# The last tile of a mixture-of-experts routing: turned once scaled, its copy shared with VectorE, four scatters moved behind the gathers, more turns of the identity

## What is computed

```python
x = x + (sigmoid(g_a) * y_attn + sigmoid(g_p) * y_pool) @ w_o
h = rmsnorm(x, g_ffn)                      # 1024 rows of 1024
logits = h @ w_router + b_router           # 32 experts
top_val, top_idx = top_k(logits, 4)        # each token goes to 4 experts
# tokens are grouped by expert; each expert's rows are gathered,
# go through gate/up, a clamped SwiGLU and down, and are added back by gate weight
```

## Time and profile before

| | |
|---|---|
| median of 3 runs | 2408.51 us (2408.11 to 2412.3) |
| the profiled execution | 2410.38 us |
| its span | 2408.7 us |
| TensorE busy | 2364.5 us, 98% of the span |
| VectorE busy | 1334.0 us, 55% |
| ScalarE busy | 460.3 us, 19% |
| GpSimd busy | 423.7 us, 18% |
| mean granted TensorE clock | 0.997 of full speed |

### The profile page before, as it was taken

How to read it: one execution, slowest core, us unless ns; L and a number is a source line. 1 busy time by engine, 2 the same in 40 slices (tenths; PEclk the granted TensorE clock), 3 DMA queues, 4 the chain that set the end, 5 groups by cost and what they waited for, 6 DMA issues and landing times. The chain is left out here.

```text
span 2408.7 us, 45402 instructions
## 1 busy us (share of the span) xinstructions
PE 2364.5 (98%) x15700; PEld 1611.2 (67%) x15700; DVE 1334.0 (55%) x2477; ACT 460.3 (19%) x1150; POOL 423.7 (18%) x589
## 2 busy tenths in 40 slices
PE   8999999999998999999999999999999999999999
PEld 6765664444444888888888888888656565555544
DVE  4665674111356654455545554556767677776565
ACT  3434552000022100000000000100212212121332
POOL 2451102121243310001100110010010101011230
PEclk9999999999999999999999999999999999999999
DMA  5000002312052798787888888888999999999462
GB/s 151 27 18 10 1 0 53 122 26 52 22 183 88 265 371 318 285 304 283 288 309 303 285 298 313 303 312 316 331 336 357 326 357 341 341 348 336 162 201 87
DMA packets 255033, 531.84 MB, mean 221 GB/s; under 512 B 17845, under 2 KB 67909, under 8 KB 254950
## 3 DMA queue, kind: packets, MB, share of 16 engines
q1 hardware_dynamic: 222302, 472.57, 55.0%
q0 software_dynamic: 17440, 38.97, 5.3%
q10 hardware_dynamic: 15208, 19.14, 2.2%
HBM read 498.76 MB, written 31.87 MB: 220 GB/s over the span
## 5 line engine op out<-in xcount | busy, mean ns | idle before, releaser
L1923 PEld LDWEIGHTS banks<-arena_a,arena_w 128*128 128x128 f32 x4608 | 562.9, 190 | 7.8 <-issue 6.5
L1923 PE MATMUL banks<-arena_a,arena_w 128*128 128x144 f32 (+7 forms) x4608 | 566.7, 286 | 1.0 <-ACT arena_a L2095 1.0
L1976 PE MATMUL banks<-arena_w,arena_a 128*64 128x256 f32 x2688 | 298.6, 380 | 3.0 <-DVE arena_a L2254 1.7
L1976 PEld LDWEIGHTS banks<-arena_w,arena_a 128*64 128x64 f32 x2688 | 193.3, 137 | 107.3 <-issue 14.1
L2349 DVE TENSOR_SCALAR arena_m<-banks,arena_m 128x160 f32<-128x160 f32 x144 | 55.3, 384 | 305.0 <-PE banks L1923 304.5
L1305 POOL DMA_DIRECT2D arena_m<-slot_tokens x32 | 18.8, 587 | 1024.9 <-issue 1024.9
L2150 ACT ACTIVATE arena_m<-arena_m 128x160 f32<-128x160 f32 x144 | 48.5, 337 | 785.7 <-DVE arena_m L2349 473.9
L1931 PE MATMUL banks<-arena_w,arena_a 128*64 128x256 f32 x1728 | 197.5, 381 | 0.0
L2032 PE MATMUL banks<-arena_w,arena_a 128*128 128x512 f32 x448 | 194.6, 592 | 0.0
L1931 PEld LDWEIGHTS banks<-arena_w,arena_a 128*64 128x64 f32 x1728 | 120.9, 137 | 67.6 <-issue 10.4
L2032 PEld LDWEIGHTS banks<-arena_w,arena_a 128*128 128x128 f32 x448 | 84.0, 190 | 100.4 <-issue 100.4
(11 more groups left out here) (410 smaller groups left out, 3443.2 us busy)
## 6 DMA issues: line engine op xcount, KB each, us to landing
arena_w<-in_w_gate_up_dram SPq DMA_DIRECT2D x128, 2048.0 KB, 12.7
arena_w<-in_w_down_dram SPq DMA_DIRECT2D x32, 4096.0 KB
expert_rows<-arena_a ACTq DMA_DIRECT2D x104, 128.0 KB, 8.6
arena_a<-in_x_dram SPq DMA_DIRECT2D x16, 512.0 KB, 4.8
arena_w<-in_w_in_dram SPq DMA_DIRECT2D x16, 512.0 KB, 5.4
arena_a<-in_b_down_dram SPq DMA_DIRECT2D x14, 512.0 KB, 15.3
expert_rows<-arena_a ACTq DMA_DIRECT2D x28, 192.0 KB
arena_a<-in_b_down_dram SPq DMA_DIRECT2D x72, 64.0 KB
```

The source lines that it names most:

```text
L1923: m = pe.matmul(GU[f % 3][:, to:to + width], w[c][:, k, at:at + P], xT[:, k, 0:width], start=(k == 0), stop=(k == K - 1), skip_group_check ...
L1976: m = pe.matmul(at[h * TH:(h + 1) * TH, :], x[:, k, :], w[:, k, h * QB:(h + 1) * QB], start=(start and k == 0), stop=(stop and k == KH - 1 ...
```

## The change

Five edits, all in the tail of routing.
1. TensorE turns the last tile (T-1) before the ranks of tile T-2, not after them.
2. For the last tile ScalarE copies only the first bank of turned rows. VectorE copies the second, between the choice and the rank of tile T-2.
3. Between the ranks of T-2 and the parts of T-1 TensorE makes ten more turns of the identity.
4. The four scatters of tile T-2 are taken out of routing's program and put behind the two gathers, together with those of T-1: two copies of token numbers, then eight indirect DMAs.
5. While the gathered rows come, TensorE makes 44 turns of the identity instead of 40.

```diff
@@ route, GpSimd
-                def scatter(n, last=False):
+                def scatter(n):
...
-                    if not last:
-                        pool.wait_ge(scattered, 64 * n + 64)
-                        pool.sem_inc(sem("dst_free"), 1)
+                    pool.wait_ge(scattered, 64 * n + 64)
+                    pool.sem_inc(sem("dst_free"), 1)
...
-                scatter(T - 2, last=True)
-
@@ route, TensorE
                 parts(T - 2)
                 logits(T - 2)
                 stay_warm(WARM // 2)
+                turn(T - 1)
                 ranks(T - 2)
-                turn(T - 1)
+                stay_warm(WARM // 4)
                 parts(T - 1)
                 logits(T - 1)
                 ranks(T - 1)
...
-                for _ in range(WARM):
+                for _ in range(WARM + WARM // 10):
                     pe.transpose(banks[0][:, 0:P], ident[:, :], ident[:, :])
@@ route, ScalarE, keep_rows
-                    for h, bank in enumerate((TB0, TB1)):
+                    for h, bank in enumerate((TB0, TB1)[:1 if n == T - 1 else 2]):
@@ route, VectorE
+                def keep_last_half():
+                    dve.wait_ge(sem("h2T_psum"), T)
+                    dve.tensor_copy(h2T[(T - 1) % 2][:, 4:8, :].rearrange("p k t -> p (k t)"), TB1[:, :]).then_inc(sem("h2T"), 1)
...
                 scale(T - 1)
                 choose(T - 2)
+                keep_last_half()
                 rank(T - 2)
                 place_rows(T - 2)
@@ experts, GpSimd
                 pool.wait_ge(route_sem("dst"), T)
-                pool.tensor_copy(tokb[1], tok[:, T - 1:T]).then_inc(sem("tokb"), 1)
-                pool.wait_ge(sem("tokb"), 1)
-                for j in range(TOP_K):
-                    pool.indirect_dma_start(list_dram, bass.IndirectOffsetOnAxis(dst[1][:, j:j + 1], 0), tokb[1], None
-                                            ).then_inc(scattered, 16)
+                for n in (T - 2, T - 1):
+                    pool.tensor_copy(tokb[n % 2], tok[:, tile_of(n):tile_of(n) + 1]).then_inc(sem("tokb"), 1)
+                pool.wait_ge(sem("tokb"), 2)
+                for n in (T - 2, T - 1):
+                    for j in range(TOP_K):
+                        pool.indirect_dma_start(list_dram, bass.IndirectOffsetOnAxis(dst[n % 2][:, j:j + 1], 0), tokb[n % 2], None
+                                                ).then_inc(scattered, 16)
                 pool.wait_ge(scattered, 64 * T)
                 pool.wait_ge(sem("table"), 32)
```

## The result

The changed kernel takes **2414.5 us** (median; 2410.46 to 2416.84), the kernel before, measured beside it, 2408.76 (2406.75 to 2412.3). The ratio is 1.0024 with a 95% interval of 1.0015 to 1.0033: it is slower by 5.7 us. The forecast was 2407.3, the range ended at 2410.3, and slower by over 0.2% had a chance of 0.04. The profiled execution takes 2413.5 us, its span is 2411.9; the mean granted clock is 0.998.

What follows compares the result with a forecast made beforehand. TensorE, busy 98%, bounds the kernel, but in routing's tail a chain of short steps over four engines does. 1.34 less 0.15 gave 1.2 us: 2408.51 - 1.2 = 2407.3 us, range 2405.2 to 2410.3.

Steps and rivals of the forecast that it cites:

- Steps 1, 2 and 3: Routing's tail: earlier turn, VectorE's half copy and ten identity turns let the last choice start 1.34 us sooner.
- rival (b): Parts of the last tile show the long lag to ScalarE's copy: gain only 0.8 us before turns, 2407.9; chance 0.2.
- Step 4: From last choice to indices nothing is removed: the 4.88 us chain moves as a whole, no clock gain counted.
- rival (d): Larger gain: clock holds through the choice (0.4 us), gather starts 0.55 sooner, turns end in time; 2406.2, chance 0.12.
- Step 5: Four scatters moved behind the gathers cost nothing, covered by GpSimd's wait for the item table and TensorE's first item.
- the step's own worst case: All scatters behind the gathers slow, landing at 812.7 us at the latest, some 2 us of the row-list wait left.
- Step 6: 44 identity turns while gathered rows come may end 0.3 us after the rows; half, 0.15 us, counted as loss.
- The sum: First expert matmul 1.2 us sooner (1.34 - 0.15), all passing through to the end: 2407.3 us.
- Whatever comes sooner at 798.98 comes sooner at the end: From the first expert matmul on, TensorE works solidly, so time won there reaches the end, and no more.
- (e): The eight scatters land so late that they reach item 1's row list: slower by several us, 2414; chance 0.03.
- (a): Clock falls again at the experts' start, in the wait for gathered rows: 2409.0, or 2412.4 if long; chance 0.15.
- (c): VectorE's copy comes at the wrong place or identity turns run over, giving back the turn's gain: 2408.5; chance 0.1.

Runs made afterwards that it cites:

- e0: The changed kernel again with no edit; 2413.75 us against 2407.75 for the kernel before, ratio 1.0026.
- e3: The changed kernel, but SyncE waits for all scatters to land before issuing the load of expert 0's second half; 2416.84 us, ratio 1.0045 to the kernel before.
- e7: The changed kernel with the item table sent by ScalarE's queue and the w_down load following at once; 2417.32 us, ratio 1.0047 to the kernel before.
- e1: The changed kernel with the four scatters of tile T-2 put back ahead of the gathers; 2410.4 us, ratio 1.0011 to the kernel before.
- e11: The kernel before with the four scatters of tile T-2 left out, only the time counts; 2406.98 us, ratio 1.0003 to the kernel before.
- e4: The changed kernel, but T-1's scatters wait until those of T-2 have landed; 2410.26 us, ratio 1.0014 to the kernel before.
- e2: The kernel before with only the scatters of T-2 moved behind the gathers; 2414.85 us, ratio 1.0032 to the kernel before.
- e5: The changed kernel with the four scatters of tile T-2 left out, only the time counts; 2404.2 us, ratio 0.9991 to the kernel before.
- e8: The changed kernel, but SyncE issues the 4 MB load without waiting for the gathered rows; 2407.84 us, ratio 1.0003 to the kernel before.
- e9: The kernel before, but SyncE issues the 4 MB load without waiting for the gathered rows; 2413.8 us, ratio 1.0030 to the kernel before.
- e10: e1 with the 4 MB load issued without waiting for the gathered rows; 2414.45 us, ratio 1.0033 to the kernel before.

## Why the prediction was wrong

**Steps 1, 2 and 3** (turn, VectorE's copy, ten turns) were right. The turn starts 0.06 us behind the scaling; VectorE's copy takes 0.68 us (0.69 forecast) and stands between choice and rank; parts to ScalarE's copy is 0.71 us, the short kind that was taken against rival (b); and the last choice starts at 780.30, directly behind the placing at 780.23, without idle time: VectorE sets it, as forecast. From the end of the scaling to that choice it is 4.63 us, and was 6.24: 1.6 us won, where 1.34 was forecast.

**Step 4**: from the choice to the indices 4.45 us (780.30 to 784.75), where 4.88 was kept. The product of the found rows took 0.61 us, at full clock. This is the 0.4 us of rival (d), and it is luck of this trace: in e0, the same kernel, the product took 0.91 us, and 1.01 or 1.02 in e3 to e7, where the clock was at half before the gathers. The 0.83 us from indices to gather stayed 0.83 with no scatter ahead of it, so it has nothing to do with them. But from the gather to the turned rows it is 5.15 us where 5.95 was taken over: a part that the sum had as fixed, and e1 and e11 show why it wasn't. It depends on the scatters in flight.

**Step 5** is the one that failed: "So this costs nothing; its cover is that wait". The step asked when the scatters would be issued and landed, and when GpSimd would next be needed. The first answer held: they were issued by 799.33 (802.5 was forecast, and the scaling ended 3.1 us sooner), and two of eight were long (1.56 and 1.31 us), which changes nothing, as it said. When they landed this trace doesn't show; they took 4.2 us from the last issue with nothing else in flight (e3: 801.02 to 805.25), but 7.95 us beside the load (e4), where 4.8 was the bound. The list still waited for the table. (In the step's own worst case the cover was 1 us and not 2, since the table was to come 1.2 us sooner too.) It didn't ask what else is in flight beside them. SyncE's 4 MB load stands there, and behind it in the same queue the table, on which the wait depends that was named as cover. So the cover was not fixed: the scatters themselves pushed its end from 14.5 to 22.7 us after the load's issue. The cost of the step, put at nothing, is 7.1 us by the medians of e2, where the tail was no shorter, and 9.2 us in the changed kernel's profile, ahead of the 2.9 won; with the four scatters gone (e5) the loss is gone. The trace of before had a sign of it that the prediction didn't read: behind T-2's scatters, when the gathers ran, the DMA share was 1.09 and 113 GB/s moved.

```profile
792.00:794.00 2.00, 2.00 (x14) 2.00 (x13) 1.86 (x13) 0.00 (x0) 1.72 (x3) 0.67 1.09 113
```


**Step 6**: the turns did run over. The rows had landed by 790.44, when SyncE, which waits for them, issued the load. TensorE took them at 790.73, directly behind the last of the 44 turns: 0.3 us lost, 0.15 forecast. In e5 more of the turns fell on the half clock, and it was 1.05 us (791.47 to 792.52), which is why its tail is longer than the changed kernel's.

**The sum** had 1.2 us for the tail; it became 2.9 in this trace, above rival (d)'s 2.3, and 1.35 to 2.6 in the others with the same tail. "Whatever comes sooner at 798.98 comes sooner at the end" was right only under a condition that the text lacked: the load moves with the tail, since it is released by the same rows, and item 1's rows hang on it with a lead of at most 1.6 us. In e5 the load is 0.8 us longer than before, and the gain passes; in e11 it is 1.1 us longer, and 0.90 us of wait appear.

**The rivals.** (e) had the edit, the sign and, at 2414, the size, with a chance of 0.03. Its mechanism was another: the scatters' own landing reaching the row list. In the trace the list is released by the table (813.13, then 4.0 us; before 811.22, then 3.8). (a) put the fall of the clock at the wait for expert 0's rows. In the changed kernel it held there and fell at item 1, behind the 4.7 us wait, for some 3.4 us, which cost about 1.7; where (a) had it, it came in e1 and e8, when the gathered rows took 7.9 and 7.7 us. (b) and (c) did not occur.

## What to carry to other kernels

A DMA that is moved isn't covered when its own landing is early enough: list everything that will be in flight beside it, above all large loads and what is queued behind them, and ask who waits for their end. Many writes of a few bytes are cheap to issue and cost the transfers that run with them; look in the DMA view for slices in which the engines are busy and the GB/s have collapsed, and see which transfer they fall on now and would fall on after the edit. And before a wait is named as cover, follow it to what ends it; if the edit can move that, it is no cover.

## What the runs showed of the hardware

- Four indirect DMAs, each of 128 numbers of 4 bytes, were followed in e4, e5 and e11 by 2 to 4 us in which the DMA engines were mostly busy and moved only some 50 to 160 GB/s instead of about 400. Where a load was well under way, the stretch began some 10 us after the first of them was issued (e4: 788.01 to 797.8; e2: 793.24 to 802.8; changed: 788.46 to 798.4). In e1 it lies at the load's start, some 7 us after. It doesn't come every time: in the kernel before the four scatters from 793.45 on are followed only by a dip to 335 GB/s at 804.4, and its load is the shortest beside scatters. Why is open. Two tiles' scatters together held a load of 4 MB down for most of its second half: 22.7 us instead of 14.5.
- The time is booked on the load, not on the small writes. Traffic by queue for 24 us from the start of the two DMA views above, packets, MB and share of 16 engines, before and then after:

```profile
q1 hardware_dynamic: 2774, 6.79, 81.9%
q0 software_dynamic: 152, 0.01, 0.5%
```
```profile
q1 hardware_dynamic: 2140, 4.20, 79.8%
q0 software_dynamic: 258, 0.00, 0.9%
```

SyncE's queue (q1) took about 80% both times, but for 4.20 MB instead of 6.79 (before, the next load falls into the 24 us); the small writes (q0) show 0.9%. Over the load's own time, 796.6 to 811.2 us before and 790.4 to 813.2 after, it is 2140 packets, 4.20 MB and 84.0% both times, in 14.6 us and in 22.8: a packet took 92 ns on average before and 143 after. The Trainium skill's page DMA: Bandwidth & Descriptors, section Back-pressure in remote DMA, says of copies between cores that stalled writes stall the source engine's other queues too. The rows here look like that, but these writes go to the core's own memory, and no run shows what stalls. Where in the DMA engines or the memory it happens stays open.
- Gathers suffer as loads do. With no scatters just ahead their rows have landed 4.9 to 5.1 us after the first gather, by the load that they release (changed, e0, e2, e5, e11); with four scatters ahead it was 6.0 (before) and 8.0 (e1), with these and the load beside them the rows were turned after 10.1 and 11.6 us (e9, e10).
